# Second block of a two-block model on one core: its fp32 projections become three products of rounded parts, on a ring of three slots and one beside it

## What is computed

```python
h = rmsnorm(x, g_pre_mix)                       # 256 x 1024
a_q, a_k, a_v, b_u, b_v, c_q, c_k, c_v = split(h @ w_in)   # 1024 x 2304
lam = exp(sum(lam_q1 * lam_k1)) - exp(sum(lam_q2 * lam_k2)) + lam_init
y_a = diff_attention(a_q, a_k, a_v, lam)        # 6 heads, two softmaxes each
y_b = spatial_gating(b_u, b_v); y_c = window_gqa(c_q, c_k, c_v)
x = x + rmsnorm(concat(y_a, y_b, y_c) @ w_out)  # 1024 x 1024
x = x + rmsnorm((silu(gate) * up) @ w_ffn_out)  # gate, up = rmsnorm(x) @ w_ffn_in, 1024 x 5632
x = x + rmsnorm((p @ w_ple_up) * sigmoid(rmsnorm(x) @ w_ple_gate))   # gate 1024 x 1024
```

## Time and profile before

| | |
|---|---|
| Runs | 1982.51, 1985.74, 1982.5 us (median 1982.51) |
| Profiled execution | 1989.03 us, span 1987.3 us |
| Granted TensorE clock, mean | 0.912 of full speed |
| PE / PEld busy | 1769.6 us (89%) / 1253.1 us (63%) |
| DVE / ACT / POOL busy | 1026.5 us (52%) / 645.6 us (32%) / 0.2 us |
| DMA | 314.91 MB, mean 158 GB/s |

### The profile page before, as it was taken

How to read it: one execution, slowest core, us unless ns; L and a number is a source line. 1 busy time by engine, 2 the same in 40 slices (tenths; PEclk the granted TensorE clock), 3 DMA queues, 4 the chain that set the end, 5 groups by cost and what they waited for, 6 DMA issues and landing times.

```text
span 1987.3 us, 18106 instructions
## 1 busy us (share of the span) xinstructions
PE 1769.6 (89%) x6987; PEld 1253.1 (63%) x6987; DVE 1026.5 (52%) x1675; ACT 645.6 (32%) x1018; POOL 0.2 (0%) x4
## 2 busy tenths in 40 slices
PE   2999889999989889899999695899998786899996
PEld 2545558888864465678887453568884554478873
DVE  7564568667746345774444327244443146254433
ACT  1022344333411223334332124343334233343433
POOL 0000000000000000000000000000000000000000
PEclk8998799999989987899999796799999895899998
DMA  8663345877555330475554431035554440135540
GB/s 323 230 218 142 106 149 180 295 262 245 213 192 213 132 115 0 159 254 190 191 185 169 126 122 63 18 135 180 177 187 145 141 148 1 66 104 190 191 159 21
DMA packets 216373, 314.91 MB, mean 158 GB/s; under 512 B 20308, under 2 KB 145628, under 8 KB 216160
## 3 DMA queue, kind: packets, MB, share of 16 engines
q1 hardware_dynamic: 216288, 313.76, 46.0%
HBM read 312.70 MB, written 1.05 MB: 158 GB/s over the span
## 4 chain that ended last, share of the span: by engine, by line
PE 79%; DVE 13%; ACT 4%; issue 3%; SPq 0%; DVEq 0%; DMA 0%; ACTq 0%
PE psum L476 17%; PE psum L483 15%; PE psum L484 15%; PE psum L485 15%; PE psum L490 6%; DVE tmp L1056 3%; DVE arena L1056 2%; ACT arena L1891 1%; PE psum L526 1%; ACT arena L1888 1%; DVE arena L1053 1%; PE psum L452 1%; PE psum L931 1%; PE psum L961 1%; DVE arena L1300 1%
## 5 line engine op out<-in xcount | busy, mean ns | idle before, releaser
L476 PE MATMUL psum<-gring,hT 128*128 128x512 f32 (+1 forms) x960 | 433.8, 611 | 17.0 <-DVE arena L1053 6.1
L485 PE MATMUL psum<-arena_parts,hT_parts 128*128 128x512 f32 x864 | 344.2, 398 | 0.0
L476 PEld LDWEIGHTS psum<-gring,hT 128*128 128x128 f32 x960 | 189.6, 201 | 237.8 <-issue 213.6
L1053 DVE TENSOR_TENSOR gring_parts<-gring,arena_parts 128x2048 fp32r<-128x2048 f32 x108 | 242.7, 2289 | 99.0 <-ACT arena_parts L1891 99.0
L483 PE MATMUL psum<-arena_parts,o_cat_parts 128*128 128x512 f32 x512 | 205.2, 401 | 7.2 <-DVE hT_parts L1053 7.2
L484 PE MATMUL psum<-gring_parts,o_cat_parts 128*128 128x512 f32 x512 | 204.4, 399 | 0.0
L1053 DVE TENSOR_TENSOR arena_parts<-psum,ex_parts 128x256 fp32r<-128x256 f32 x108 | 45.3, 420 | 303.8 <-ACT ex_parts L1891 303.8
L1891 ACT ACTIVATE arena_parts<-gring 128x2048 fp32r<-128x2048 f32 x108 | 200.6, 1915 | 0.8 <-DMA gring<-in_w_up 0.7
L485 PEld LDWEIGHTS psum<-arena_parts,hT_parts 128*128 128x128 f32 x864 | 164.8, 191 | 39.1
L483 PE MATMUL psum<-arena_parts,ex_parts 128*128 128x512 f32 x432 | 180.4, 417 | 0.0
L1891 ACT ACTIVATE ex_parts<-psum 128x256 fp32r<-128x256 f32 x108 | 41.3, 382 | 416.2 <-PE psum L526 416.2
(11 more groups left out here) (207 smaller groups left out, 1889.7 us busy)
## 6 DMA issues: line engine op xcount, KB each, us to landing
gring<-in_w_ada SPq DMA_DIRECT2D x24, 2048.0 KB, 10.1
gring<-in_w_ffn_in SPq DMA_DIRECT2D x44, 1024.0 KB, 7.6
gring<-in_w_gate SPq DMA_DIRECT2D x32, 1024.0 KB, 7.5
gring<-in_w_up SPq DMA_DIRECT2D x32, 1024.0 KB, 9.9
dring<-in_w_down SPq DMA_DIRECT2D x32, 1024.0 KB, 5.1
gring<-in_w_in SPq DMA_DIRECT2D x14, 2048.0 KB, 10.8
dring<-in_w_ffn_out SPq DMA_DIRECT2D x22, 1024.0 KB, 4.9
gring<-in_w_out SPq DMA_DIRECT2D x8, 2048.0 KB, 8.8
```

Source lines behind the costliest of these rows:

```text
L476: last = nc.tensor.matmul(ps[:, 0:n], hT[:, k, t * P:(t + 1) * P], w[:, k, 0:n], start=k == 0, stop=k == KT - 1)
L485: return nc.tensor.matmul(ps, lo, w, start=False, stop=stop)
L1053: return nc.vector.tensor_tensor(o, a, b, op)
```

## The change

1. The ring has three slots. A slot beside it, `side`, takes the ada chunks that are loaded between the experts (`load_aside`, each waiting for the one before to be reduced). The other ada chunks stay in the ring.
2. In the second block all projections (avcv, aq, ak, buv, cqk, wo, pg) become three fp32r products per k-tile (`chunk_tokens`, `chunk_features`). ACT rounds each chunk in two halves (`rounded_chunk`) into `side`, into `dring` or into the part of the arena that holds rounded expert weights, as the table ROUNDED says. The rest is written in place by DVE (`chunk_rest`), for wo0 and wo1 by GpSimd (`pool_second`).
3. The activations are taken apart too: `hT` and `hT3` by a copy of ACT and a subtraction of DVE, the transposed mix in the same way straight from PSUM.
4. avcv comes first. That of b0 is loaded, rounded and subtracted during the last experts of a1, that of b1 during the PLE gate of b0. At the entry of b0, DVE norms the first tile for the second block before it finishes the second tile of the first block.
5. The rounding of gu1 stands behind the two `modulated_T` in ACT's queue of the first block. dn0 and dn1 of a second-block layer are loaded after the last product of wo, as `dring` holds rounded chunks until then.

```diff
-GS = 4
+GS = 3
...
+ROUNDED = {
+    ("b", 0): {"avcv": "side", "aq": "down", "ak": "side", "buv": "down", "cqk": "side", "wo0": "down", "wo1": "side",
+               "pg0": "side", "pg1": "arena"},
+    ("b", 1): {"avcv": "down", "aq": "side", "ak": "down", "buv": "side", "cqk": "down", "wo0": "side", "wo1": "down",
+               "pg0": "side", "pg1": "arena"},
+}
...
+        def rounded(stage, name):
+
+            place = ROUNDED[stage][name]
+            if place == "side":
+                return side_hi
+            if place == "down":
+                return dring_rest.rearrange("p s f n -> p (s f n)").rearrange("p (k n) -> p k n", k=KT)
+            return w_hi[1]
...
+        def rounded_before(stage, name):
+
+            place = ROUNDED[stage][name]
+            if place == "side":
+                before, used = SIDE[SIDE.index((stage, name)) - 1]
+                return before, *last_use(before, used)
+            if place == "arena":
+                return stage, T, ("gu1", NF - 2)
+            earlier = [n for n, p in ROUNDED[stage].items() if p == "down"]
+            if earlier.index(name):
+                return stage, *last_use(stage, earlier[earlier.index(name) - 1])
+            return (FIRST[-1], T, ("dn1", NE - 1)) if stage == SECOND[0] else (SECOND[0], T, ("e", 1, 1))
...
+        def chunk_tokens(stage, ps, t, name, hi, first, ks=range(KT), n=N):
+
+            w, w_rest = rounded(stage, name), g_rest(stage, name)
+            for k in ks:
+                if first and k % 4 == 0:
+                    wait_weights(name, k // 4)
+                last = split_product(ps[:, 0:n], hi[:, t, k, :], h_lo[:, k, t * P:(t + 1) * P], w[:, k, 0:n], w_rest[:, k, 0:n], k == 0, k == KT - 1)
+            return last
...
+        def chunk_features(stage, ps, name, hi, c0, at, first):
+
+            w, w_rest = rounded(stage, name), g_rest(stage, name)
+            o = ps[:, at:at + SEQ].rearrange("p (t n) -> p t n", t=TT)
+            for k in range(KT):
+                if first and k % 4 == 0:
+                    wait_weights(name, k // 4)
+                nc.tensor.matmul(o, w[:, k, c0:c0 + P], hi[:, :, k, :], start=k == 0, stop=False)
+                nc.tensor.matmul(ps[:, at:at + SEQ], w[:, k, c0:c0 + P], h_lo[:, k, :], start=False, stop=False)
+                last = nc.tensor.matmul(o, w_rest[:, k, c0:c0 + P], hi[:, :, k, :], start=False, stop=k == KT - 1)
+            return last
...
+            for t in range(TT):
+                wait_parts("hT", t)
+                chunk_tokens(stage, bank(T, ("avcv", t)), t, "avcv", h_hi[1], t == 0).then_inc(tensor_done, T.step(("avcv", t)))
             for name in ("aq", "ak"):
                 features(name, 0, 2)
                 features(name, 1, 1)
-            tokens("avcv", 0)
...
+        def chunk_rest(stage, name, n=N):
+
+            for q in range(2):
+                k = slice(q * KT // 2, (q + 1) * KT // 2)
+                dve.wait_ge(scalar_done, A.of(stage, ("hi", name, q)))
+                tt(g_rest(stage, name)[:, k, 0:n], gslot(stage, name)[:, k, 0:n], rounded(stage, name)[:, k, 0:n], ALU.subtract).then_inc(vector_done, V.step(("lo", name, q), stage))
...
+            def joined(t):
+                dve.wait_ge(tensor_done, T.of(FIRST[-1], (f"dn{t}", NE - 1)))
+                for h in range(2):
+                    residual(psum[:, 4 + 2 * t + h, :], t, h, ("read", ("out", t, h)))
+                moments("in", t)
+
+            def scaled(t):
+                normed("in", t)
+                dve.wait_ge(rows_loaded, rows_count(FIRST[-1]))
+                gain_and_bias(t, ("x", "in", t))
+
             if l == 0:
-                for t in range(TT):
-                    dve.wait_ge(tensor_done, T.of(FIRST[-1], (f"dn{t}", NE - 1)))
-                    for h in range(2):
-                        residual(psum[:, 4 + 2 * t + h, :], t, h, ("read", ("out", t, h)))
-                    moments("in", t)
-                    normed("in", t)
-                    dve.wait_ge(rows_loaded, rows_count(FIRST[-1]))
-                    gain_and_bias(t, ("x", "in", t))
+                joined(0)
+                scaled(0)
+                joined(1)
             pre_norm("mix", 0)
+            if l == 0:
+                scaled(1)
             modulated("xT", "hT", 0, g_mix)
+            features_rest("hT", 0, h_hi[1])
             pre_norm("mix", 1)
             modulated("xT", "hT", 1, g_mix)
+            features_rest("hT", 1, h_hi[1])
+            chunk_rest(stage, "aq", 384)
+            chunk_rest(stage, "ak", 384)
...
+            chunk_rest(stage, "buv")
             for s in range(3):
                 diff_in(s)
             dve.wait_ge(vector_done, V.now())
             for s in range(len(DIFF)):
+                if s == 0:
+                    chunk_rest(stage, "cqk")
                 if s == 4:
                     gate_moments()
...
+            for g in range(KT // 2):
+                dve.wait_ge(scalar_done, A.at(V, ("oThi", g)))
+                ps = bank(V, ("oT", g)).rearrange("p (f t n) -> p f t n", f=2, t=TT)
+                for f in range(2):
+                    k = 2 * g + f
+                    tt(h_lo[:, k, :].rearrange("p (t n) -> p t n", t=TT), ps[:, f], h_hi[1][:, :, k, :], ALU.subtract).then_inc(vector_done, V.step(("oTlo", g) if f else None))
+                V.also(("read", ("oT", g)))
...
+        def rounded_chunk(stage, name, n=N):
+
+            act.wait_ge(G.sem(stage, name), G.level(stage, name))
+            before, done, mark = rounded_before(stage, name)
+            act.wait_ge(done.sem, done.of(before, mark))
+            act.sem_inc(waited)
+            for q in range(2):
+                k = slice(q * KT // 2, (q + 1) * KT // 2)
+                copy(rounded(stage, name)[:, k, 0:n], gslot(stage, name)[:, k, 0:n]).then_inc(scalar_done, A.step(("hi", name, q), stage))
...
             rounded_weights(0)
+            for t in range(TT):
+                root_of("mix", rstd[:, t:t + 1], t)
+                modulated_T("xT2", "hT2", t, *folded["ffn"], hi=h_hi[0])
             rounded_weights(1)
...
+            rounded_chunk(stage, "ak", 384)
+            for t in range(TT):
+                tokens("avcv", avcv, t)
             for b in range(2):
                 features("aq", qT2, b, 2 - b, DQK ** -0.5)
+            rounded_chunk(stage, "buv")
             for b in range(2):
                 features("ak", kT2, b, 2 - b)
+            rounded_chunk(stage, "cqk")
             act.wait_ge(vector_done, V.at(A, "lsum"))
             activate(lsum, lsum, ACT.Exp).then_inc(scalar_done, A.step("lexp"))
             act.wait_ge(scalar_done, A.now())
-            for t in range(TT):
-                tokens("avcv", avcv, t)
             parameters_T()
...
+                if s == 3:
+                    rounded_chunk(stage, "wo0")
+                if s == 6:
+                    rounded_chunk(stage, "wo1")
...
-                ps = bank(A, ("oT", g))
-                copy(hT[:, 2 * g:2 * g + 2, :].rearrange("p f n -> p (f n)"), ps).then_inc(scalar_done, A.step(("oTc", g)))
-                act.wait_ge(scalar_done, A.now())
-                A.also(("read", ("oT", g)))
+                ps = bank(A, ("oT", g)).rearrange("p (f t n) -> p f t n", f=2, t=TT)
+                for f in range(2):
+                    copy(h_hi[1][:, :, 2 * g + f, :], ps[:, f]).then_inc(scalar_done, A.step(("oThi", g) if f else None))
...
+            def gate_weights(e):
+                if e == NF - 2:
+                    rounded_chunk(stage, "pg0")
+
+            act_experts(NF, 1, gate_weights)
...
+                if t == 0:
+                    rounded_chunk(stage, "pg1")
+            if l + 1 < DEPTH:
+                rounded_chunk(SECOND[l + 1], "avcv")
...
+        def pool_second(l):
+            stage = SECOND[l]
+            Q.begin(stage)
+            for name in BY_POOL:
+                for q in range(2):
+                    pool.wait_ge(scalar_done, A.at(Q, ("hi", name, q)))
+                    for k in range(q * KT // 2, (q + 1) * KT // 2):
+                        nc.gpsimd.tensor_tensor(g_rest(stage, name)[:, k, 0:N], gslot(stage, name)[:, k, 0:N], rounded(stage, name)[:, k, 0:N], ALU.subtract).then_inc(pool_done, Q.step(("lo", name, q) if k % 4 == 3 else None))
...
+        def load_aside(stage, name):
+
+            if SIDE.index((stage, name)):
+                before, used = SIDE[SIDE.index((stage, name)) - 1]
+                sp.wait_ge(vector_done, V.of(before, ("acc", used)))
+                sp.sem_inc(waited)
+            load(side[:, :, 0:N], by_row(w[:, c * N:(c + 1) * N]), side_landed)
```

207 lines of the change are left out of this document (124 added, 83 removed).

## The result

| | before | after |
|---|---|---|
| Runs | 1982.5 to 1985.74 us, median 1982.66 | 2015.96, 2016.48, 2019.93, 2023.95 us, median 2018.2 |
| Profiled execution, span | 1989.03, 1987.3 us | 2015.96, 2014.1 us |
| Ratio of the runs | | 1.018 (95%: 1.0155 to 1.0205) |
| PE, DVE, ACT, POOL busy | 1769.6, 1026.5, 645.6, 0.2 us | 1738.4, 1120.3, 717.8, 41.4 us |

Slower, as forecast, but by 35.5 us where 13.3 was predicted; 2018.2 lies above the range of 1968 to 2008. The two traces differ by 26.8 us in span. Where the time went is read from the traces.

The account below looks back on a forecast made before the run. PE products were taken as three quarters of the chain, with DVE and ACT bounding between attention heads. First block +12.3, b0 -0.9, b1 +1.9 us gave +13.3: median 1982.5 to 1995.8 us, 8-in-10 range 1968 to 2008.

Parts of the forecast that it names:

- (a): Layer a0: ada9's load must wait for mvo's ring slot, so DVE starts reducing it later; +6.7 us.
- (b): Layer a1: ada5's load waits for a ring slot and lands after it is needed; +3.6 us.
- (c): First block's router: ACT rounds gu1 before its table load and sigmoid; +1.0 us in each of two layers.
- (d): Entry of second block: DVE's finishing of the first block's second tile leaves the path; -2.7 us in b0, +0.1 in b1.
- (e): Attention's first half: shorter products, but cqk's late load and rounding stall PE some 9 us; +0.9 at b0's fifth head.
- (f): Attention heads: ACT rounds wo0 after head 3 and wo1 after head 6, delaying probabilities; +3.3 us, bounds 0 and 7.7.
- (g): Mixed heads before wo: two ACT copies and two DVE subtractions replace one copy; +2.4 us.
- (h): wo's four products fall to 5.5 us each, the norm and transpose chain between them unchanged; -3.8 us.
- (i), (j): pg0's rest in the last feed-forward chunk, +0.3 us; then pg's last three products in 16.5 us instead of 20.61, -4.0.
- fourth rival: New idle time slows PE's clock and GpSimd (POOL) slows DVE: 2005.4 us, 2011 with contention; chance 0.15.
- Rival 1: PE stays the bound in the attention's first half, cqk landing early: 13.3 us per layer better, 1969.2 us; chance 0.15.
- second rival: PE-bound everywhere: products shrink by 26 us per layer, ACT's roundings absorbed; 1947.6 us; chance 0.05.

Follow-up runs that it names:

- experiment 7: Changed kernel with GpSimd's rests on DVE, ada9/ada5 beside the ring, lam and buv's rest first, avcv's rounding inside expert 14, and wo's roundings moved: 1955.73 us, ratio 0.9838.
- Experiment 9: Changed kernel with only avcv's rounding moved, between the two hidden tiles of expert 14: 2010.33 us, ratio 1.0128.
- Experiment 4: Changed kernel with lam's exponential and buv's rest first, cqk's rounding after three heads' exponentials, its rest after the first head's join: 1986.46 us, ratio 1.0001.
- experiments 8 and 10: The first: changed kernel with wo in fp32, 1998.45 us. The second: that plus avcv's rounding moved, ada9/ada5 beside the ring, lam and buv's rest first, 1955.8 us.

## Why the prediction was wrong in size

The direction and most of the steps were right; two costs were put at nothing in the sum. They hold 16.6 us, more than the 13.5 by which the traces exceed the sum; the other steps together came in 3 lower. Point by point, in the working's letters, forecast and measured, in us of the traces:

| step | forecast | measured |
|---|---|---|
| (a) ada9 | +6.7 | +4.8 |
| (b) ada5 | +3.6 | +3.6 |
| (c) router, two layers | +2.0 | +0.3 |
| avcv in the last experts | 0 | +6.0 |
| (d) entry of b0 | -2.7 | -2.9 |
| (e) first product to the seventh head | +3.6 | +2.5, +3.0 |
| (f) two roundings | +3.3 | +3.2, +3.0 (experiment 7: 3.1) |
| GpSimd's rests | 0 | +5.3 per layer |
| (g) parts of the mix | +2.4 | +2.0, +2.0 |
| (h) wo | -3.8 | -0.5, -3.3 |
| (i), (j) feed-forward and pg, in b0 to b1's first product, in b1 to the end | -3.7 | -3.9, -3.3 |

**The step that failed first** is the sentence on avcv, "PE, the bound there, waits for neither". I asked whether ACT had time for the rounding, and it has, 8.1 us in each expert. I did not ask when the chunk lands: it is issued at 1060.4, behind the wait of dn14, and ACT stands at its head 5 us before it lands, with the next expert's activation behind it. The working even named the price if the cover failed, one rounding of 3.8; measured it is 6.0, the wait of 4.8 and the rounding of 3.7, less slack, and then products at the lower clock. Experiment 9 shows it: the same instructions at another place in the same queue cost nothing.

**The second** is GpSimd's rests. They were in the fourth rival, bounded at 3 us per layer, and in the sum at nothing. The row that would have priced it, a DVE operation beside a GpSimd one, is not in the trace of before; from the rows of after it is about 0.9 us on each TENSOR_SCALAR and on each short operation with two inputs in SBUF, of which 2.6 us per chunk reach the chain. The bound in the rival was drawn from the sentence of the Trainium skill on contention ("GPSIMD Engine Reference", specifications). The trace bears out that the operations with two SBUF inputs suffer; my price was too small. What is added, 0.98, 0.88 and 0.95 us, hardly depends on the length of the operation, 0.35, 0.48 and 0.44, so it looks like a wait and not like a slower rate.

**(h)** was mis-sized: 0.5 and 3.3 us were gained where 3.8 was forecast. The chain of norms lets the fourth product's transposes begin 8.7 us after the end of the second product, before as after. The third product, which lies in that time, is now shorter, so PE idles for 3.1 us in both layers and not for 1.9, and behind the idle time the clock is lower. The stretches of the changed kernel in b0: first two products, third, and the fourth behind its transposes.

```profile
1290.24:1303.41 13.17, 13.17 (x49) 10.62 (x50) 4.49 (x2) 3.09 (x4) 0.00 (x0) 0.85 0.01 1
1303.41:1308.97 5.56, 5.56 (x24) 4.14 (x23) 2.97 (x6) 2.17 (x4) 0.00 (x0) 1.00 0.00 0
1312.11:1321.51 9.40, 9.40 (x33) 7.84 (x34) 2.42 (x6) 2.98 (x8) 0.00 (x0) 0.68 0.50 168
```

The third product is 5.56 us, as worked out from the split products. The fourth and its transposes take 9.40 at a clock of 0.68, where in the kernel before they took 7.94 at 1.00. The same 56 instructions from the transposes on, in the changed kernel's b1 and b0, and in b0 of experiment 7, where the same wait of 3.1 us was followed by full clock:

```profile
1758.99:1772.51 13.52, 13.51 (x56) 10.94 (x56) 5.53 (x12) 4.97 (x13) 0.00 (x0) 0.90 0.69 227
1312.11:1327.05 14.94, 14.94 (x56) 11.98 (x56) 5.52 (x12) 4.97 (x13) 0.00 (x0) 0.80 0.59 203
```

```profile
1276.36:1288.57 12.21, 12.21 (x56) 9.73 (x56) 5.53 (x12) 4.86 (x13) 0.00 (x0) 1.00 0.72 248
```

So the lower clock costs 1.3 and 2.7 us there. It is no accident of one trace: the eight transposes behind this wait take 1.9 us in 16 of the 18 layers in which wo is three products (nine kernels), and 1.07 in the other two, b0 of experiments 4 and 7. In all six layers with wo in fp32 (the kernel before, experiments 8 and 10) the wait is 1.9 us and the transposes take 1.07. Why the clock stayed up in two is open. The rest of the difference between b0 and b1 lies partly in the kernel before, whose first three products of wo took 22.3 us in b0 and 23.5 in b1.

**What was right, and where that was luck.** The queue of (e) came as laid out: the first scores 44.1 us after the first product (43.8 forecast), behind cqk's rounding, lam and buv's rest, with PE idle for 9.7 us. Two errors cancel in it. cqk was issued 20.8 us after the first product and not 22.9, since the two products of avcv lost 1.1 us to the lower clock, where 2.6 were reckoned, and aq's blocks were shorter: 24 fp32r products of 256 columns take 2.84 us in a row, 0.355 us per k-tile, and not the 0.385 of the router's. And it landed 13.1 us after its issue and not 10.8: the earlier trace rows are the loads in one piece, and cqk comes in seven. Whether fewer pieces would shorten the wait was not tried. Nor was PE's idle time ended by DVE, as the signs had it, but by ACT's copies.

Rival 1 was refused for the right reason, a landing far above 6 us. Experiment 4 shows that its 13.3 us per layer were near (12.4 by the traces), not through a quicker landing, on which I had made it hang, but through the order of two queues behind the same landing. The second rival's 26 us per layer do not follow from the rows: twelve token products at 1.4 us and ten blocks of features at 0.4 make 21, and PE's busy time fell by 16 per layer. Both halves of the fourth rival came in part: GpSimd's, and new idle time with a lower clock, in the last experts and in wo; the mean granted clock fell from 0.912 to 0.897. Its 2011 was the tail that I left out of the range, and the median of 2018.2 lies beyond that too. The estimate of 0.645 us per k-tile for three products rests on the four passes that the Trainium skill ("FP8 and Floating Point Precision", TensorE Precision Notes) gives for true fp32, and on one pass for reduced fp32, which I worked out from its being cut to FP22 there. The third product of wo, 0.695 us per k-tile at full clock, stands against it.

The median's distance remains. By the traces it is 26.8 us, by the runs 35.5 with an interval of 31 to 41. So of the 22 us by which the median missed, the steps above explain 13.5, and 8.7 are where the two profiled executions lie among their kernels' runs. The runs of before fall into two groups: of 33 on record, 19 took 1982.4 to 1983.5 us, 13 took 1987.4 to 1991.6, and one 1985.74; the profiled one, 1989.03, is of the upper group, and the median that the result is measured against of the lower. The traces show where executions part: DVE's step that came at 123.77 in the kernel before came at 120.42 to 124.21 in the others, behind the same work, and in a1 equal products ran at different clocks (experiment 9). What decides it was not measured.

## What to carry to other kernels

When work is put into an engine's idle time, look at when its input lands and at what stands behind it in the same queue, not at the idle time alone: the same rounding of 3.7 us cost 6.0 us at one place of ACT's queue and nothing a half expert later, and one queue order around a late load was worth 12 us per layer. An engine that was idle is not free either; price what its accesses do to the engine beside it. Look at how many pieces a load has before taking a landing time for it. And a product that gets shorter pays only if what follows it was waiting for it: pg's did, wo's did not.

## What was not expected of the hardware

While GpSimd ran its subtractions of 128x512 (1.29 us each, 10.3 for eight, against 4.5 for DVE's two halves of the same chunk), DVE's TENSOR_SCALAR of 128x256 went from 0.35 to 1.33 us and its SCALAR_TENSOR_TENSOR between SBUF operands from 0.48 to 1.36, nearly one GpSimd instruction more each, while the one that read PSUM and a TENSOR_REDUCE with one SBUF input stayed at 0.69. The Trainium skill ("GPSIMD Engine Reference", specifications) says that the two engines share SBUF interfaces, with contention for DVE's two-port modes and for two SBUF inputs. For two inputs the rows agree, and the size is theirs; in which mode the TENSOR_SCALAR ran no row shows.
